# Routing weights stationary on four column groups with a folding matmul, and the copies of modulation chunk 4 placed ahead of the last key copies

## What is computed

```python
mod = silu(cond) @ w_mod[i] + b_mod[i]        # 6 x 1024, for each of 2 conditions
shift1, scale1, gate1, shift2, scale2, gate2 = split(mod)
h = rms_norm(x, norm1_g[i]) * (1 + scale1) + shift1
x = x + gate1 * mix(h)                        # attention, then @ w_out
h = rms_norm(x, norm2_g[i]) * (1 + scale2) + shift2
g_prob = softmax(h @ w_grp + b_grp)           # 4 groups
e_logits = h @ w_rtr + b_rtr                  # 16 experts: 20 columns with the groups
# best group, its two best experts, weights from the softmaxes
x = x + gate2 * experts(h)
```

## Time and profile before

| | |
|---|---|
| runs | 1418.89, 1421.32, 1426.35 us; median 1421.32 |
| profiled execution | 1422.78 us, of which the span from first to last instruction is 1420.6 |
| TensorE | 1261.5 us busy (89%) |
| VectorE | 717.2 us (50%) |
| ScalarE | 410.5 us (29%) |
| GpSimd | 212.0 us (15%) |
| DMA | 245.19 MB moved, mean 173 GB/s |
| routing matmuls (L2075) | 160 records, 19.2 us busy |
| modulation matmuls (L1773) | 1536 records, 49.5 us busy |
| mean granted TensorE clock | 0.955 of full speed |

### The profile page before, as it was taken

How to read it: one execution, slowest core, us unless ns; L and a number is a source line. 1 busy time by engine, 2 the same in 40 slices (tenths; PEclk the granted TensorE clock), 3 DMA queues, 4 the chain that set the end, 5 groups by cost and what they waited for, 6 DMA issues and landing times. The chain is left out here.

```text
span 1420.6 us, 22599 instructions
## 1 busy us (share of the span) xinstructions
PE 1261.5 (89%) x8192; PEld 752.9 (53%) x8192; DVE 717.2 (50%) x1727; ACT 410.5 (29%) x923; POOL 212.0 (15%) x305
## 2 busy tenths in 40 slices
PE   4999989999999959998959999899999994999981
PEld 3455556777767734433435554577776773444330
DVE  0344436777734535544514553466785346455452
ACT  2111145666610111111111111666664000111111
POOL 1210021010021111121111010210101111122212
PEclk9899999999999979999979999999999996999995
DMA  9700288010041796999950005850002224899965
GB/s 348 293 14 1 79 293 223 1 32 16 1 163 61 276 390 224 356 371 374 311 172 14 0 1 178 288 130 1 32 16 99 110 102 155 313 375 377 328 207 180
DMA packets 73707, 245.19 MB, mean 173 GB/s; under 512 B 6071, under 2 KB 14752, under 8 KB 60976
## 3 DMA queue, kind: packets, MB, share of 16 engines
q1 hardware_dynamic: 56080, 183.26, 34.7%
q0 software_dynamic: 17056, 58.61, 14.1%
q10 hardware_dynamic: 432, 1.36, 0.2%
HBM read 213.87 MB, written 31.00 MB: 172 GB/s over the span
## 5 line engine op out<-in xcount | busy, mean ns | idle before, releaser
L1856 PE MATMUL ps<-ring,hT_region 128*128 128x512 f32 (+1 forms) x640 | 271.2, 580 | 3.4 <-ACT hT_region L957 3.4
L1856 PEld LDWEIGHTS ps<-ring,hT_region 128*128 128x128 f32 x640 | 121.2, 193 | 134.9 <-issue 134.4
L1321 DVE TENSOR_SCALAR_CACHE_REDUCE ring<-ps 128x768 f32<-128x768 f32 (+1 forms) x168 | 132.7, 820 | 107.1 <-PE ps L1930 85.1
L1010 ACT ACTIVATE ring<-ring,negm 128x768 f32<-128x768 f32 (+1 forms) x168 | 137.6, 820 | 26.8 <-DVE ring L1321 26.8
L2055 PE MATMUL ps<-ring,hT_region 128*128 128x384 f32 (+1 forms) x480 | 141.9, 452 | 0.0
L2197 PE MATMUL ps<-ring,hT_region 128*128 x272 | 129.6, 633 | 10.3 <-SPq L590 4.4
L1930 PE MATMUL ps<-arena,qT 64*128 64x384 f32 (+1 forms) x640 | 124.8, 507 | 6.2 <-DVE ring L1321 2.9
L2055 PEld LDWEIGHTS ps<-ring,hT_region 128*128 128x128 f32 x480 | 89.6, 190 | 42.0 <-issue 0.3
L1983 PE MATMUL ps<-work,arena 128*64 128x128 f32 x1600 | 105.0, 278 | 5.6 <-ACT work L1026 4.3
L1026 ACT ACTIVATE work<-ps 128x512 f32<-128x512 f32 x128 | 75.8, 592 | 98.0 <-PE ps L1748 98.0
L1983 PEld LDWEIGHTS ps<-work,arena 128*64 128x64 f32 x1600 | 85.9, 136 | 24.6 <-issue 14.3
(11 more groups left out here) (297 smaller groups left out, 1750.1 us busy)
## 6 DMA issues: line engine op xcount, KB each, us to landing
ring<-in_w_mod SPq DMA_DIRECT2D x24, 2048.0 KB, 9.4
ring<-in_moe_w_gate SPq DMA_DIRECT2D x32, 1024.0 KB, 11.4
ring<-in_moe_w_up SPq DMA_DIRECT2D x32, 1024.0 KB, 15.0
arena<-in_moe_w_down SPq DMA_DIRECT2D x32, 1024.0 KB, 13.5
ring<-in_w_in SPq DMA_DIRECT2D x6, 2048.0 KB, 21.2
arena<-mod_rows POOLq DMA_DIRECT2D x12, 512.0 KB, 5.7
x_rows<-x POOLq DMA_DIRECT2D x10, 512.0 KB, 3.0
h_rows<-work POOLq DMA_DIRECT2D x10, 512.0 KB, 2.9
```

The costliest lines, as they stand in the source:

```text
L1010: act.activation(v, v, ACT.Exp, bias=negm[:, 2 * (k % 3) + m:2 * (k % 3) + m + 1], scale=-1.0, accum_out=sums[:, c:c + 1]).then_inc(exp_do ...
L1321: ts(o_, i_, -pair_of(p)[4], None, ALU.mult, ALU.min, accum_out=col).then_inc(m_ready, 1)
L1856: last = mm(ps[:, b, 0:n], hT[:, c, t * P:(t + 1) * P], w[:, c, :], start=(c == 0), stop=(c == KC - 1))
```

## The change

1. The routing of tiles 0 to 3 is turned round: 32 columns of the weights are stationary (20 of them, and 12 of the next channel block, whose results are not used), the 128 transposed token columns move. The 8 channel blocks go to four column groups, g = c % 4, each writing 32 partitions of bank 6, columns 0 to 127; two blocks are added in each group. The result has logits on partitions and tokens on columns, in four partial sums.
2. ScalarE copies this 128x128 result to SBUF (`part_copy`, behind `x2T_copy`). `router_sum` on TensorE then multiplies it, stationary, with a constant `fold` (128x20, the four 32-row groups of an identity laid over each other): this adds the four partial sums and transposes in one. The result is in bank 6, columns 128 to 147. It stands behind `out_block(t, 2)`; for tile 3 between `last_T(0)` and `out_block(4, 2)`.
3. `logits_in` of tiles 0 to 2 moves on VectorE behind the third residual block, that of tile 3 behind the scaling of the last tile. The copies of the next transposed tile wait for the new matmuls (`rp_done`) where they waited for the router.
4. `fold` is computed once, on VectorE, in layer 0 at the start of the last tile's attention (one reduction).
5. `mod_copy(l, 4)` on ScalarE moves from behind the query copy to ahead of the last key copies; chunks 5 and 6 stay.
6. Three counters (`s_modbias`, `s_fill`, `s_final`) become one, `s_once`, with the sums of their counts (128 for the first two, 144 with the last).

The diff, cut to its core:

```diff
@@ -200,6 +200,7 @@
         ones_b = sb("ones_b", P, BF16)
         rope = sb("rope", NT * 96)
         sel64 = sb("sel64", 2)
+        fold = sb("fold", 20)
         cond = sb("cond", KC * 2)
         cond_e = sb("cond_e", KC * 2)
         silu_c = sb("silu_c", KC * 2)
...
@@ -264,9 +265,12 @@
         oT = hT
         x2T = work[:, 0:1024].rearrange("p (c n) -> p c n", c=KC)
         h2 = work[:, 1024:2048]
+        rt_part = work[:, 2432:2560]
+        rt_sum = ps[:, 6, 128:148]
         junk2 = qT[:, D:2 * D]
         col2rows = k_tok[0:4 * KC, 256:256 + P]
         w_rt2 = [v.rearrange("p (c n) -> p c n", c=KC) for v in (k_tok[:, 384:544], k_tok[:, 896:1056])]
+        w_rt32 = [[k_tok[:, at + 20 * c:at + 20 * c + 32] for c in range(KC)] for at in (384, 896)]
         b_rt2 = k_tok[:, 544:584].rearrange("p (k n) -> p k n", k=2)
         prod2 = k_tok[:, 1056:1216].rearrange("p (n c) -> p n c", c=KC)
         part2 = k_tok[:, 1216:1256]
...
@@ -987,6 +991,7 @@
                     if t + 1 < NT:
                         hT_copy(t + 1)
                     z_copy_last(t)
+                mod_copy(l, MOD_FIRST)
                 key_copies_a(l, NU - 1)
                 key_copies_b(l, NU - 1)
 
...
@@ -1032,7 +1037,7 @@
                                    ps[:, 7, :].rearrange("p (c n) -> p c n", c=4), ACT.Copy).then_inc(o_evac, 1)
 
                 query_copy(0)
-                for j in range(MOD_FIRST, MOD_FIRST + MOD_EARLY):
+                for j in range(MOD_FIRST + 1, MOD_FIRST + MOD_EARLY):
                     mod_copy(l, j)
                 for k in range(NP + 4):
                     t, p = divmod(k, N_PR)
...
@@ -1068,13 +1073,20 @@
                 def x2T_copy(t):
                     act.wait_ge(x2T_done, l * 2 * (NT - 1) + 2 * t + 2)
                     if t >= 1:
-                        act.wait_ge(rt_done, l * NT + t)
+                        act.wait_ge(rp_done, l * (NT - 1) + t)
                     act.activation(x2T[:, 4:8, :], ps[:, 7, :].rearrange("p (c n) -> p c n", c=4),
                                    ACT.Copy).then_inc(x2T_evac_a, 1)
+
+                def part_copy(t):
+                    act.wait_ge(rp_done, l * (NT - 1) + t + 1)
+                    if t >= 1:
+                        act.wait_ge(rt_done, l * NT + t)
+                    act.activation(rt_part, ps[:, 6, 0:P], ACT.Copy).then_inc(rp_evac, 1)
 
                 for t in range(NT - 1):
                     norm2_sums(t)
                     x2T_copy(t)
+                    part_copy(t)
 
                 act.wait_ge(lastT_done, 3 * l + 2)
                 act.activation(x2T[:, 3:6, :], ps[:, 5, 0:384].rearrange("p (c n) -> p c n", c=3),
...
@@ -1389,6 +1401,8 @@
                     stt(a2col, col2[:, :, 1, :], 1.0, n2col.unsqueeze(1).to_broadcast([P, 2, KC]), ALU.add, ALU.mult)
                     dve.drain()
                     w = w_rt[:].rearrange("p (c n) -> p c n", c=KC)
+                    if l == 0:
+                        red(fold[:], ident[:].rearrange("p (g n) -> p n g", g=4)[:, 0:20, :], AX.X, ALU.add)
                     for q in range(2):
                         tt(w_rt2[q], w, a2col[:, q, :].unsqueeze(2).to_broadcast([P, KC, 20]), ALU.mult)
 
...
@@ -1477,20 +1491,20 @@
                 def x2T_copy(t):
                     dve.wait_ge(x2T_done, l * 2 * (NT - 1) + 2 * t + 1)
                     if t >= 1:
-                        dve.wait_ge(rt_done, l * NT + t)
+                        dve.wait_ge(rp_done, l * (NT - 1) + t)
                     cp(x2T[:, 0:4, :], ps[:, 6, :].rearrange("p (c n) -> p c n", c=4)).then_inc(x2T_evac_d, 1)
 
                 def last_copy(n):
                     c0, c1, at = ((0, 3, 4), None, (6, 8, 7))[n]
                     dve.wait_ge(lastT_done, 3 * l + n + 1)
-                    dve.wait_ge(rt_done, l * NT + NT - 1)
+                    dve.wait_ge(rp_done, (l + 1) * (NT - 1))
                     cp(x2T[:, c0:c1, :], ps[:, at, 0:(c1 - c0) * P].rearrange("p (c n) -> p c n", n=P)
                        ).then_inc(last_evac_d, 1)
 
                 def logits_in(t):
                     dve.wait_ge(rt_done, l * NT + t + 1)
                     dve.wait_ge(rs2_ready, l * NT + t + 1)
-                    stt(logits[:, t, :], ps[:, 6, 0:20], rs2[:, t:t + 1], b_rt2[:, min(t, 1), :], ALU.mult, ALU.add
+                    stt(logits[:, t, :], rt_sum if t + 1 < NT else ps[:, 6, 0:20], rs2[:, t:t + 1], b_rt2[:, min(t, 1), :], ALU.mult, ALU.add
                         ).then_inc(lg_ready, 1)
 
                 for t in range(NT):
...
@@ -1503,12 +1517,13 @@
                     x_add(t, 1)
                     if t == 1:
                         normalise(NT - 1)
-                    if t >= 1:
-                        logits_in(t - 1)
                     if t == NT - 1:
                         last_copy(0)
                         scale_last(0, WO_COLS[2][0])
+                        logits_in(t - 1)
                     x_add(t, 2)
+                    if 1 <= t < NT - 1:
+                        logits_in(t - 1)
                 last_copy(2)
                 scale_last(*WO_COLS[2])
                 logits_in(NT - 1)
...
@@ -2070,9 +2085,20 @@
                             last = tr(ps[:, 6 + r, q * P:(q + 1) * P], x_t[t][:, c * P:(c + 1) * P])
                         last.then_inc(x2T_done, 1)
 
-                def router(t, c0, c1):
+                def router_parts(t):
+                    for c in range(KC):
+                        g = c % 4
+                        last = mm(ps[32 * g:32 * g + 32, 6, 0:P], w_rt32[min(t, 1)][c], x2T[:, c, :],
+                                  start=(c < 4), stop=(c >= 4))
+                    last.then_inc(rp_done, 1)
+
+                def router_sum(t):
+                    pe.wait_ge(rp_evac, l * (NT - 1) + t + 1)
+                    mm(rt_sum, rt_part, fold[:], start=True, stop=True).then_inc(rt_done, 1)
+
+                def router_last(c0, c1):
                     for c in range(c0, c1):
-                        last = mm(ps[:, 6, 0:20], x2T[:, c, :], w_rt2[min(t, 1)][:, c, :],
+                        last = mm(ps[:, 6, 0:20], x2T[:, c, :], w_rt2[1][:, c, :],
                                   start=(c == 0), stop=(c == KC - 1))
                     if c1 == KC:
                         last.then_inc(rt_done, 1)
...
@@ -2097,19 +2123,22 @@
                     if t >= 1:
                         pe.wait_ge(x2T_evac_d, l * (NT - 1) + t)
                         pe.wait_ge(x2T_evac_a, l * (NT - 1) + t)
-                        router(t - 1, 0, KC)
+                        router_parts(t - 1)
                     if t == NT - 1:
                         last_T(0)
+                        router_sum(t - 1)
                     out_block(t, 2)
+                    if 1 <= t < NT - 1:
+                        router_sum(t - 1)
                 last_T(1)
                 pe.wait_ge(lg_ready, l * NT + NT - 1)
                 pe.wait_ge(last_evac_d, 2 * l + 1)
-                router(NT - 1, 0, 3)
+                router_last(0, 3)
                 last_T(2)
                 pe.wait_ge(last_evac_a, l + 1)
-                router(NT - 1, 3, 6)
+                router_last(3, 6)
                 pe.wait_ge(last_evac_d, 2 * l + 2)
-                router(NT - 1, 6, KC)
+                router_last(6, KC)
 
                 pe.wait_ge(xo_done, l * 15 + 15)
                 if l + 1 < DEPTH:
```

More of the change, by code:

```diff
@@ L364, in trunk @@
         x_final = sem("x_final")
-        s_fill = sem("s_fill")
-        s_final = sem("s_final")
+        s_once = sem("s_once")
         s_yleft = sem("s_yleft")
@@ L418, in trunk @@
         rt_done = sem("rt_done")
+        rp_done = sem("rp_done")
+        rp_evac = sem("rp_evac")
         lg_ready = sem("lg_ready")
@@ L741, in _ @@
             for rows_ in (h_rows, *x_rows):
-                dma(rows_[0:P, :], a["x_prompt"][0]).then_inc(s_fill, 16)
+                dma(rows_[0:P, :], a["x_prompt"][0]).then_inc(s_once, 16)
             dma(lane_w[0:N_ET, :], row_b(a["step_tables"].rearrange("k m e -> (k m e)"), N_TAB * 2 * NE, N_ET)
-                ).then_inc(s_fill, 16)
+                ).then_inc(s_once, 16)
             small_load(pool, 0, 2)
@@ L748, in _ @@
                 for k in range(2):
-                    dma(mod_rows[l, k], a["b_mod"][l]).then_inc(s_modbias, 16)
+                    dma(mod_rows[l, k], a["b_mod"][l]).then_inc(s_once, 16)
             for l in range(DEPTH):
                 if l == 0:
-                    pool.wait_ge(s_modbias, 64)
+                    pool.wait_ge(s_once, 128)
                 for t in range(NT):
@@ L833, in _ @@
                 if l == 0:
-                    pool.wait_ge(s_fill, 64)
+                    pool.wait_ge(s_once, 128)
                 def y_store(i):
@@ L886, in _ @@
                 rsqrt(rsf[:, t:t + 1], ssf[:, t:t + 1], 1).then_inc(f_rs, 1)
-            pool.wait_ge(s_final, 16)
+            pool.wait_ge(s_once, 144)
```

(2 more changed lines are left out.)

5 lines of the change are left out of this document (2 added, 3 removed).

## The result

The changed kernel takes 1417.82 us (median of 20 runs, 1410.97 to 1423.41); the kernel before, run beside it, 1426.03 us (20 runs, 1418.89 to 1430.83). The ratio is 0.9942, 95% interval 0.9926 to 0.9959: **8.2 us faster**, 5.8 to 10.5. The forecast was a gain of 10.2 us and a time of 1411.1 (1406 to 1417); the time lies 0.8 us above that range. Of the 6.7 us between forecast and result, 4.7 are the base: three runs of the kernel before had a median of 1421.32, twenty (these three among them) have 1426.03. The other 2.0 are the gain; the interval of the measured gain still holds the forecast 10.2. The profiled execution after took 1415.01 us, its span is 1413.3, the mean granted clock 0.950 (before 1422.78, 1420.6, 0.955).

The account below looks back on a forecast made before the run. TensorE's queue was taken to bound the output stage, and its wait ahead of chunk 6 the start of attention. Routing 6.6 plus copies 3.8 less 0.2 for VectorE's reduction gave 10.2 us, from 1421.3 to 1411.1 us; range 1406 to 1417.

Parts of the forecast that it names:

- Routing: Output stage, routing of tiles 0 to 3: turned matmuls and fold shorten TensorE's queue by 3.3 us a layer, 6.6 in all.
- (a): Output stage, per tile: eight matmuls on four column groups, 16 records at 27.3 ns plus 0.11 fixed, 0.55 us.
- Rival (A): Routing matmuls: column groups cost 0.94 us a tile, as on two groups at L2004; 3.1 us less gain, 1414.2; chance 0.09.
- rival (D): Routing matmuls wait for each other's loads, 138 ns a record; kernel 4.0 us slower than before, 1425.3; chance 0.03.
- (b): Output stage, per tile: TensorE going back from column groups to the whole array costs 0.10 us.
- (c): Output stage, per tile: the folding matmul, 128 stationary and 20 moving columns, 2 records of 107 ns, 0.21 us.
- The last tile: Routing of tile 3 with the last tile's first transposes: fold waits for ScalarE's copy; 2.07 us become 1.42, 0.65 saved.
- Copies: Start of attention: chunk 4's copies move earlier, ending TensorE's 1.91 us wait ahead of chunk 6 in both layers; 3.8 us.
- Rival (C): Start of attention: moving chunk 4's copies gives nothing, since keys or queries get late in turn; 1414.9; chance 0.07.
- The base: Whole kernel: gain taken from the median of three runs, 1421.3, not the profiled 1422.78; 1411.1 where the profile gives 1412.6.
- It should move as a whole: Expert stage behind the routing: tied to it by waits, so it passes on the gain; no loss reckoned.
- Rival (B): Expert stage: clock's rise shifts about 3 us a layer; half the gain lost, 1416, or the good way 1407; chance 0.17.

Follow-up runs that it names:

- e13: Changed kernel with 240 instructions more at TensorE's start, nearly all behind a branch never taken; 0.9903 of the kernel before, 13.8 us faster.
- e18: The same kernel as e13, run again: changed kernel with 240 instructions that never run; 0.9928 of the kernel before, 10.3 us faster.
- e14: Kernel before with the new routing alone, plus 240 instructions at TensorE's start, nearly all behind a branch never taken; 0.994 of the kernel before.
- e2: Kernel before with the new routing alone, copies of modulation chunk 4 left behind the query copy; 0.9994 of the kernel before, 0.9 us faster.
- e5: Kernel before with 16 instructions of already met waits at TensorE's start; 1.0022 of the kernel before, 3.1 us slower.
- e15: Kernel before with 16 instructions more at TensorE's start, by a branch that is never taken; 0.9996 of the kernel before.
- e16: Kernel before with 256 instructions more, a whole piece, at TensorE's start, by a branch that is never taken; 0.998 of the kernel before.
- e9: Changed kernel with 240 instructions of met waits, 165 at TensorE's start and 75 later in layer 0, ahead of the change of layers; 0.9949 of the kernel before.

## Why the prediction was right or wrong

**Bounds of the kernel: right.** In the output stage every microsecond taken from TensorE's queue came off the stage, and nothing there got late.

**Routing: right, 3.17 us a layer for 3.3.** (a) The matmuls on column groups: 0.57 to 0.58 us from start to start, forecast 0.55, some 36 ns a record. Rival (A) with 0.94 and rival (D), which needed 109 ns a record, fall. With them falls the rule of the Trainium skill (TensorE: Matmul & The Clock Gate, Part 3) as the prediction used it: these sixteen share their row groups and have a load each, and run at 36 ns. (b) The change of mode: 0.20 us, 0.10 on each side, where (b) has 0.10 and (a) a fixed 0.11. The Trainium skill (TensorEngine Tiling, Key Properties) says that a change of tiling mode drains TensorE; the trace agrees, with these 0.10 us on each side. (c) The fold: 0.14 us behind a block where 0.21 was forecast. A middle tile then has 0.57 + 0.20 + 0.14 = 0.91 for the forecast 0.86 and saves 0.78 (16.43 - 15.65), forecast 0.85. The last tile: 1.29 us where 1.42 was forecast. The fold did wait for ScalarE's copy there, but it could start at 1.05 (1169.44 - 1168.39), where the prediction has the copy at 1.10, and took 0.24 from there to the next block where 0.32 was reckoned.

**Copies: right, 1.9 and 1.6 us, 4.6 us (1.9 to 7.4) when timed alone.** Rival (C) falls.

**The base: wrong.** The sum was made against the profile (1412.6) and then set down by 1.5 us to the median of three runs. Twenty runs put that median 4.7 us higher. The same gain of 10.2 from 1426.03 is 1415.8, inside the range. Executions of one kernel spread over 12 us here (1418.89 to 1430.83), while the three runs spread over 7.5; the range's ends were made from costs of the change, and had next to no room for the base. This step alone puts the time outside the range: with the gain as measured, 8.2, the old base would give 1413.1.

**"It should move as a whole": wrong for what lies behind the expert stage.** With this sentence the sum put everything behind the routing at nothing, and this is the step that failed in the gain. The expert stage did move as a whole (first gate and up to last down matmul 198.95 us before, 198.99 after; over all profiles the mean is 198.7 with the old routing and 198.4 with the new). The change of layers behind it didn't: 2.6 us are lost there in the mean by the place of TensorE's code. The mechanism was in none of the rivals. Rival (B) had a loss of about 3 us for what lies behind the routing, but by the clock in the expert stage, and the equal lengths speak against that. The sum with the missing term is 10.2 - 2.6 = 7.6 us, and 8.2 (5.8 to 10.5) was measured; with the code a whole piece further, 12.1 was measured for 10.2 forecast. Both intervals of that kernel, e13 and e18, hold the 10.2 too, and so does that of the 8.2, so the missing term rests on the traces and on e14 against e2, not on these sums. The late packets belong to the place and not to the routing: with the same routing and the code 240 further they aren't there, and with the old routing and the code 16 further they are.

## What to carry to other kernels

Take the base from many runs or from a wide interval: three runs of a kernel that scatters by 12 us can miss its median by more than the change is worth. Where an engine jumps over code (unused tiles, branches) on the path, instructions that are added ahead of it count by their place too. Look for a wait on the engine's own sequencer and for instruction packets in it, put the packets' times on the clock of the instructions before comparing them, and try it with instructions behind a branch that is never taken, not with waits that run. And when two chains end in one place, price the third before adding their gains.

## What the runs showed of the hardware

- Code comes in packets of 16,384 bytes. While TensorE jumps over unused tiles the last two start 3.0 to 3.4 us apart or, with the code 16 instructions further, 5.1 to 6.1, and TensorE goes on 2.6 to 3.5 us behind the last. 256 instructions more restore the pattern and add one packet (53 ahead of the restart for 52), which fits 64 bytes an instruction. The packets' queue doesn't name its engine; that they are TensorE's follows from e5, e13, e15 and e16, which change TensorE's program alone.
- A wait that is already met is not free on TensorE: 165 instructions of two waits each took 21.6 us (e9), 0.13 us an instruction.
- Sixteen fp32 records with 32 stationary columns on four column groups run at 36 ns each, loads included. Going to column groups and back costs 0.10 us on each side.
- The granted clock drops in the first tile of attention in some profiles, whichever kernel it is (in e15, the kernel before with 16 instructions that never run, it is 0.58 from 206 to 209 us). The changed kernel in windows of 3 us (us, busy us (x) of PE, PEld, DVE, ACT, POOL, PEclk, DMA, GB/s):

```profile
200.00:203.00 3.00, 1.81 (x31) 1.08 (x21) 1.02 (x8) 2.76 (x13) 2.37 (x4) 1.00 1.02 380
203.00:206.00 3.00, 2.77 (x38) 1.72 (x40) 1.02 (x8) 2.52 (x12) 0.85 (x2) 0.78 1.05 391
206.00:209.00 3.00, 3.00 (x54) 1.85 (x44) 0.21 (x1) 0.56 (x3) 0.00 (x0) 0.65 1.05 386
209.00:212.00 3.00, 2.85 (x28) 1.66 (x26) 1.32 (x12) 2.96 (x14) 1.60 (x2) 1.00 1.03 364
```

Part of that time is at the lower of the two levels, 1.2 GHz, and attention of layer 0 is 1.6 us longer than before (198.84 and 197.22). TensorE was busy for 1.81 of 3 us in the window ahead of the fall and for 2.77 in the one in which it fell. It isn't the change: eleven profiles with the early copies have a mean of 198.8 us for this stage, nine without them 198.7, both from 197.2 to over 201. What decides it in an execution stays open.
